# Stacked scores, packed values and a moved projection in the attention round of a two-block kernel

## What is computed

```python
h = xn @ w_in
b_c, c_c, h_c, q, k, v, g_conv, g_attn = jnp.split(h, list(splits), axis=-1)
y_conv = b_c * causal_dwconv(c_c * h_c, conv_w_mix)
...
# stick-breaking attention: 16 heads of 64, strictly causal
z = jnp.einsum("bqhd,bkhd->bhqk", qb, kb) * scale
log_beta = jax.nn.log_sigmoid(z)
log_fail = jnp.where(causal, log_beta - z, 0.0)
survive = lax.cumsum(log_fail, axis=3, reverse=True) - log_fail
a = jnp.where(causal, jnp.exp(log_beta + survive), 0.0)
o = jnp.einsum("bhqk,bkhd->bqhd", a, vb)
```

## Time and profile before

| | us |
|---|---|
| median of 3 runs (lowest to highest) | 1988.21 (1986.0 to 1995.19) |
| the profiled execution | 1980.69 |
| its span in the trace | 1979.0 |
| PE busy in the span | 1809.9 (91%) |
| DVE, ACT, POOL busy | 1096.1 (55%), 883.7 (45%), 227.3 (11%) |
| the eight rounds, first score to the last gap of the stage | 53.3 to 521.1 |

### The profile page before, as it was taken

The page is one execution under the profiler, slowest core; times in us unless marked ns, Lnnn a source line. Parts: engine busy times, 40 slices in busy tenths (PEclk is TensorE's granted clock), DMA queues, the critical chain, the costliest instruction groups (busy, mean ns, idle before and its releaser), DMA issues.

```text
span 1979.0 us, 31110 instructions
## 1 busy us (share of the span) xinstructions
PE 1809.9 (91%) x11965; PEld 1597.1 (81%) x11965; DVE 1096.1 (55%) x1580; ACT 883.7 (45%) x1157; POOL 227.3 (11%) x347
## 2 busy tenths in 40 slices
PE   5999999999999996999999968477879999999996
PEld 4899999999999995899888836366657777778884
DVE  4455445555333347554542277999677767654543
ACT  4565665666433344333332233134455565643332
POOL 0011111010000010000000007687000000000001
PEclk8999899999999998999999989799989999999998
DMA  3222122222223261232233228211202122133332
GB/s 121 77 83 67 53 85 74 75 74 83 63 90 95 90 197 43 88 95 95 85 98 96 93 101 139 38 40 46 76 22 86 59 74 69 48 106 112 123 101 96
DMA packets 64721, 166.02 MB, mean 84 GB/s; under 512 B 21956, under 2 KB 22148, under 8 KB 64520
## 3 DMA queue, kind: packets, MB, share of 16 engines
q1 hardware_dynamic: 64648, 165.03, 27.8%
HBM read 154.23 MB, written 8.41 MB: 82 GB/s over the span
## 4 chain that ended last, share of the span: by engine, by line
PE 71%; DVE 20%; ACT 4%; issue 3%; DMA 1%; SPq 0%; DVEq 0%; ACTq 0%; POOL 0%
PE J L749 32%; PE J L986 13%; PE J L761 6%; PE J L957 6%; PE J L866 3%; PE Z L821 2%; DVE WL L1687 2%; PE J L1153 2%; PE Z L833 1%; DVE VR L1963 1%; DVE VI L1963 1%; PE J L1104 1%; PE ZT L777 1%; DVE TS L1963 1%; DVE MX L2227 1%
## 5 line engine op out<-in xcount | busy, mean ns | idle before, releaser
L1687 DVE TENSOR_TENSOR WL<-WR,WH 128x1024 fp32r<-128x1024 f32 x271 | 337.3, 1245 | 328.8 <-ACT WH L1232 319.3
L1232 ACT ACTIVATE WH<-WR 128x1024 fp32r<-128x1024 f32 x271 | 285.6, 1055 | 220.8 <-DMA WR<-weights 76.0
L749 PE MATMUL J<-XH,WH 128*128 128x264 f32 (+1 forms) x1376 | 285.8, 289 | 22.9 <-DVE XL L1691 18.8
L749 PE MATMUL J<-XL,WH 128*128 128x264 f32 (+1 forms) x1376 | 281.4, 286 | 0.0
L749 PE MATMUL J<-XH,WL 128*128 128x264 f32 (+1 forms) x1376 | 281.0, 286 | 0.0
L749 PEld LDWEIGHTS J<-XH,WH 128*128 128x128 f32 x1376 | 217.4, 191 | 27.8 <-issue 17.1
L749 PEld LDWEIGHTS J<-XL,WH 128*128 128x128 f32 x1376 | 216.4, 191 | 0.0
L749 PEld LDWEIGHTS J<-XH,WL 128*128 128x128 f32 x1376 | 215.6, 191 | 0.0
L2371 POOL TENSOR_TENSOR SA<-SQ 128x512 f32<-128x512 f32 (+1 forms) x3 | 3.9, 1295 | 1018.4 <-ACT SQ L1463 511.4
L2352 POOL TENSOR_SCALAR_AFFINE_SELECT E<-E 128x128 f32<-128x128 f32 (+1 forms) x160 | 50.9, 354 | 460.1 <-DVE E L1754 246.5
L986 PE MATMUL J<-X2H,WH 128*128 128x512 f32 x168 | 70.8, 421 | 11.1 <-DVE X2L L2008 8.8
(11 more groups left out here) (435 smaller groups left out, 4334.5 us busy)
## 6 DMA issues: line engine op xcount, KB each, us to landing
WR<-weights SPq DMA_DIRECT2D x271, 512.0 KB, 3.5
X<-tokens SPq DMA_DIRECT2D x4, 528.0 KB, 5.5
H<-tokens SPq DMA_DIRECT2D x8, 264.0 KB, 4.2
res_dram<-H SPq DMA_DIRECT2D x1, 2048.0 KB, 8.1
u_dram<-UT SPq DMA_DIRECT2D x8, 256.0 KB, 2.2
US<-u_dram SPq DMA_DIRECT2D x16, 128.0 KB, 7.2
gate_dram<-GST SPq DMA_DIRECT2D x8, 256.0 KB, 2.2
GSB<-gate_dram SPq DMA_DIRECT2D x8, 256.0 KB, 3.7
```

The lines of the kernel that those rows point to most:

```text
L749: mm = pe.matmul(o[:, 512 * h:512 * h + half], ws[:, s, w], xs[:, a:a + half], start=(k == 0 and i == 0), stop=(k == 7 and i == 2))
L1232: act.activation(WH[:, n % SPLIT, :], WR[:, n % RAW, :], ACT.Copy).then_inc(w_hi, 1)
L1687: dve.tensor_tensor(WL[:, n % SPLIT, :], WR[:, n % RAW, :], WH[:, n % SPLIT, :].bitcast(F32), ALU.subtract).then_inc(w_lo, 1)
```

## The change

It does four things.

**Scores.** q's high and low half are stacked on the partitions of one operand per head (QS, 128 rows), k's high half is written twice (KS, 128 rows), so one pass gives high by high + low by high. A second pass over 64 rows adds the low half of k. 12 matmuls per head in place of 18, all of the first pass ahead of all of the second.

**Values.** The high and low half of a head's v stand side by side in one stationary operand (VW), so that the upper 64 output rows hold the low part. 18 matmuls per head in place of 27. The two halves of the output have to be added: ACT copies the one to OT (`head_part`), DVE adds the other (`head_sum`), ACT makes OH from OT, and DVE OL (`head_lo`).

**Copies.** q is read out by two instructions of 64 rows on ACT and two on DVE, k by four on ACT and two on DVE, where each was one.

**Order.** PE does job, then values(h-1); and job q, then values(h), then job k. The turns are: q t + 10, values(h) t + 11, k t + 12; in the first half the job has t + 5 and values(h-1) t + 6. On ACT and DVE the readers follow: q is read out before the values, both after `softplus(h + 1)`.

```diff
-                for kt, t0, w, c in PIECES:
-                    for ks, qs in ((KH, QH), (KH, QL), (KL, QH)):
-                        mm = pe.matmul(Z[:, c:c + w], ks[r, kt * P:(kt + 1) * P], qs[r, t0:t0 + w],
-                                       start=c // 512 not in banks, stop=True, skip_group_check=True)
-                        banks.add(c // 512)
+                    mm = pe.matmul(Z[:, c:c + w], KS[h % 2][:, kt * P:(kt + 1) * P], QS[h % 2][:, t0:t0 + w],
+                                   start=c // 512 not in banks, stop=True, skip_group_check=True)
+                    banks.add(c // 512)
+                for kt, t0, w, c in PIECES:
+                    mm = pe.matmul(Z[:, c:c + w], KL[r, kt * P:(kt + 1) * P], QS[h % 2][r, t0:t0 + w],
+                                   start=False, stop=True, skip_group_check=True)
...
-                    for vs, ps in ((VH, AH), (VH, AL), (VL, AH)):
-                        mm = pe.matmul(o[:, at + a:at + b], vs[:, kt * P:(kt + 1) * P], ps[:, c + a:c + b],
+                    for ps in (AH, AL):
+                        mm = pe.matmul(o[:, at + a:at + b], VW[:, kt, h % 2].rearrange("p x d -> p (x d)"), ps[:, c + a:c + b],
...
                 scores(h)
+                job(n + 1, t + 5, XH, XL)
                 if m.base or m.reg is not None:
-                    values(h - 1, t + 5)
-                job(n + 1, t + 6, XH, XL)
+                    values(h - 1, t + 6)
+                pe.wait_ge(read_out[slot(t + 4)], nth(t + 4) + 1)
                 turn_values(t + 7)
...
                 scores(h + 1)
+                if last:
+                    job(n + 6, t + 10, XH, XL, start=LIVE, half=HALFK)
+                else:
+                    job(n + 6, t + 10, XH, XL)
                 pe.wait_ge(read_out[slot(t + 7)], nth(t + 7) + 1)
-                values(h, t + 10)
+                values(h, t + 11)
                 if last:
-                    job(n + 6, t + 11, XH, XL, start=LIVE, half=HALFK)
                     job(n + 7, t + 12, XH, XL, start=LIVE, half=HALFK)
                 else:
-                    job(n + 6, t + 11, XH, XL)
                     job(n + 7, t + 12, XH, XL)
```

More of the change, by code:

```diff
@@ L175, in t_gate @@
     m = as_lin(m)
-    return T_GATE + (-1, 0, 1, 3)[j] if m.reg is None and m.base == 0 else T_GATE + 4 * m + j
+    return T_GATE + (-2, 0, 1, 3)[j] if m.reg is None and m.base == 0 else T_GATE + 4 * m + j
 def t_zs(m):
@@ L204, in halves, with heads @@
     return ap.rearrange("p (h t) -> p h t", h=2)
+def heads(ap):
+    return ap.rearrange("p (k x d) -> p k x d", x=2, d=64)
 def build(nc, weights, cond, params, tokens, bmat, cmat, positions, out):
@@ L580, in stream, with store_mod @@
                 repeat(sp, (last - first) // RAW, 1, lambda i: load_weights(first + RAW * i))
-            def store_mod(first, width, done):
+            def store_mod(first, width, done, rows=MROW):
                 sp.wait_ge(mod_rows, val(done))
-                sp.dma_start(mod_dram[:, cols(first, width)], MROW[0:2, 0:width]).then_inc(mod_saved, 16)
+                sp.dma_start(mod_dram[:, cols(first, width)], rows[0:2, 0:width]).then_inc(mod_saved, 16)
             def load_row(n, row):
@@ L1247, in _ @@
             act.activation(NONE[:], STAGE[:, 1, :], ACT.Copy, scale=-1.0).then_inc(const_r, 1)
-            act.activation(KH[:, L1:], STAGE[:, 1, 0:KPAD - L1], ACT.Copy, scale=0.0).then_inc(zeroed_act, 1)
+            act.activation(KS0[:, L1:], STAGE[:, 1, 0:KPAD - L1], ACT.Copy, scale=0.0).then_inc(zeroed_act, 1)
             act.activation(KL[:, L1:], STAGE[:, 1, 0:KPAD - L1], ACT.Copy, scale=0.0).then_inc(zeroed_act, 1)
@@ L1266, in _ @@
             root(0)
+            act.activation(KS[1][:, L1:], STAGE[:, 1, 0:KPAD - L1], ACT.Copy, scale=0.0).then_inc(zeroed_act, 1)
             for m in range(DT):
@@ L1365, in mix @@
                 softplus(h + 1)
-                head_out(h, m, t + 10)
+                if not last:
+                    q_hi(m + 1, t + 10, n + 6)
+                head_part(h, t + 11)
                 fail_hi(h + 1)
+                head_out(h, m, t + 11)
                 if not last:
-                    q_hi(m + 1, t + 11, n + 6)
                     split_hi(n + 10)
@@ L1737, in q_lo @@
                 dve.wait_ge(qk_hi, val(2 * m + 1))
-                dve.scalar_tensor_tensor(out=halves(QL[:]), in0=JV[as_lin(t) % 2], scalar=0.125,
-                                         in1=halves(QH[:]).bitcast(F32),
-                                         op0=ALU.mult, op1=ALU.subtract).then_inc(read_out[as_lin(t) % 2], 1)
+                for x in range(2):
+                    r, other = slice(64 * x, 64 * x + 64), slice(64 - 64 * x, P - 64 * x)
+                    ins = dve.scalar_tensor_tensor(out=halves(QS[x][other]), in0=JV[as_lin(t) % 2][r], scalar=0.125,
+                                                   in1=halves(QS[x][r]).bitcast(F32), op0=ALU.mult, op1=ALU.subtract)
+                ins.then_inc(read_out[as_lin(t) % 2], 1)
             def k_lo(m, t):
+                dve.wait_ge(k_first, val(m + 1))
+                low(halves(KL[0:64, 0:L1]), JV[as_lin(t) % 2][0:64], halves(KS[0][0:64, 0:L1]))
                 dve.wait_ge(qk_hi, val(2 * m + 2))
-                low(halves(KL[:, 0:L1]), JV[as_lin(t) % 2], halves(KH[:, 0:L1])).then_inc(read_out[as_lin(t) % 2], 1)
-            q_lo(0, T_MIX + 1)
+                low(halves(KL[64:P, 0:L1]), JV[as_lin(t) % 2][64:P], halves(KS[1][64:P, 0:L1]))\
+                    .then_inc(read_out[as_lin(t) % 2], 1)
+            q_lo(0, T_MIX)
             split_lo(SPLIT)
@@ L1835, in mix @@
                 low(YL[:, cols(m * L1, L1)], CT[:], YH[:, cols(m * L1, L1)]).then_inc(y_lo, 1)
-                head_out(h, m, t + 10)
+                if not last:
+                    q_lo(m + 1, t + 10)
+                head_sum(h, t + 11)
                 fail_lo(h + 1)
+                head_lo(h, m)
                 if not last:
-                    q_lo(m + 1, t + 11)
                     split_lo(n + 10)
```

93 lines of the change are left out of this document (58 added, 35 removed).

## The result

| | before | changed |
|---|---|---|
| median of the runs, us | 1990.31 (4 runs, 1986.0 to 1995.19) | 2013.82 (4 runs, 2007.49 to 2017.42) |
| ratio to before, 95% interval | | 1.0117 [1.0088, 1.0146] |
| span of the profiled execution, us | 1979.0 | 2005.5 |
| mean granted clock of TensorE in it | 0.968 | 0.957 |

The changed kernel is 1.2% slower: 23.5 us in the medians, 26.5 us between the two profiled spans. The forecast was 2001 us with a range up to 2012, so the sign was right and the size too small: the measured median lies 2 us above the range.

A forecast was written before the change was run, and what follows sets the result against it. PE, busy throughout the rounds, was taken to bound the kernel; its savings would become idle time before job k. 1980.7 + 0.6 (rounds, edges) + 12 (clock) = 1993.3 us profiled; as median 1988.2 + 12.6 = 2000.8, stated as 2001, range 1986 to 2012.

The forecast's parts named there:

- first round: First round of the stage: CT gap and low clock go, 59.45 to 57.4 us, -2.0; clock loss behind job k's gap added.
- LL and k's four copies: Around accumulate: LL stays hidden by 1 to 2 us, k's copies by 0.1 to 0.4, otherwise some 0.3 us a round.
- the forecast's two rows, of 2.64 and 2.81 us: Profiled gaps on PE before the change: clock fell behind 2.64 us, losing 1.7 us, but stayed at 1.00 behind 2.81.
- the single gap of 1.48 us: PE's wait for the first KL before the change: clock stayed at 1.00, so nothing was added for small idle times.
- Edges (b): Start: PE's 1.48 us wait for the first KL grows by three copies of 0.5 us, +1.4.
- softplus(h+1) starts at 321.15 + 0.1: Fifth round on ACT: softplus stays behind YH, only 0.1 us later, though its scores finish 3 us earlier.
- round +0.2: Each round: job k starts at 330.3 against 330.13, so the round takes 57.2 us; five undisturbed rounds, +1.0.
- the clock, 1.7 us in seven of eight: Behind the gaps ahead of job k: low clock costs 1.7 us each in seven of eight, +12 us; bounds none and 20.
- Rival 3: Worse: low stretches cost 2.5 us each, k's copies come out behind accumulate, (d) is not hidden; 2016 us, chance 0.12.
- (d): Third round: clock at 0.50 for 9.5 us without a gap cost 4.7; job k's gap absorbs it, -4.4.
- Last round: Second gate job waits for the first gate's sigmoid, +4.3; the stage's last gap adds +0.3, together +4.6.
- Rival 4: Faster: softplus(h+1) follows its scores, not YH; 1968 us, or 1957 if job k never waits for q; chance 0.11.

The follow-up runs named there:

- Experiments 2, 3 and 5: Groups of runs: 2 took order and forms apart (e3_order_alone, e4); 3 moved softplus or q's readout (e5, e2); 5 removed the wait (e7, e8).
- e2: Changed kernel with q read out in the middle of softplus(h+1), ahead of its last pass, on ACT and DVE; 1994.45 us, ratio 1.0018.
- experiment 1: Changed kernel with 30, 15 or 22 unused matmuls filling the wait before job k (e1, e11_fill_15, e12); 1999.64, 1995.4 and 2000.2 us.
- e11_fill_15: Changed kernel with 15 unused matmuls between values(h) and job k in each round; 1995.4 us in one execution.
- e4: Changed kernel's stacked scores and packed values in the order, turns and places of the kernel before; 1979.19 us, ratio 0.9940.
- e6_start: Changed kernel with the program's first q put in the other tile, as before the change; 2007.41 us, ratio 1.0086.
- e1: Changed kernel with 30 unused matmuls between values(h) and job k in each round; 1999.64 us, ratio 1.0050.
- e5: Changed kernel with ACT's copy of y (YH) put behind softplus(h+1); 2002.15 us, ratio 1.0049.
- e12: Changed kernel with 22 unused matmuls between values(h) and job k in each round; 2000.2 us in one execution.
- e3_order_alone: Kernel before with only the new order and turns, keeping its old three-pass scores and values; 2001.24 us, ratio 1.0037.
- e8: Changed kernel with e7's order and tiles, plus y put behind softplus and q's readout on ACT and DVE; 1952.08 us, ratio 0.9792.
- e9: e8's order with the kernel before's forms: three-pass scores and values and the old readouts; 1975.59 us, ratio 0.9917.
- e7: Changed kernel with q and k in different tiles, values(h) behind both, and the first gate's sigmoid directly behind softplus; 1964.14 us, ratio 0.9853.
- e10: e8 with packed values alone: scores back to three passes with the old copies of q and k; 1964.95 us, ratio 0.9864.

## Why the prediction was right in its mechanism and wrong in its size

Its terms against the two profiled executions, in us; the kernel's stage is cut at the same matmuls in both:

| part | forecast | measured |
|---|---|---|
| start, to the first scores (53.34 to 59.38) | +1.4 | +6.0 |
| first round (59.46 to 59.35) | -0.3 | -0.1 |
| rounds 2 to 7 (346.72 to 359.57) | +6.8 | +12.85 |
| last round to the last gap (61.59 to 68.69) | +4.6 | +7.1 |
| sum | +12.6 | +25.9 |

Of the 13.3 us missed, 4.6 lie at the start, 6.1 in rounds 2 to 7 (4.0 of it the chain to job k, the rest mostly the clock) and 2.5 in the last round, where it is all clock.

**Right.** Job k waits for q's readout behind softplus(h+1), PE idles from 37.8 us of the round (forecast 37.6), and what PE saved lies in that wait. Experiments 2, 3 and 5 show the cause: without the forms the wait is 0.9 us with the same round at full clock, with q's readout earlier (e2) job k begins earlier, and without the shared tile the wait is gone and so is the loss. LL and k's four copies stayed hidden: there is no gap behind accumulate. The clock falls behind these gaps, and experiment 1 shows what that is worth by itself. The Trainium skill's oscillation rule (TensorE: Matmul & The Clock Gate, "HAM oscillation — how this bites in real kernels"), by which every burst behind a wait starts cold, agrees with all seven waits of 4.2 to 4.8 us here; the six of 2.8 to 3.0 us in e11_fill_15 did not do it. The waits that the section describes are longer than those six, so neither they nor the forecast's two rows, of 2.64 and 2.81 us, tell for or against it. The Trainium skill's second rule, in the section "A second HAM failure mode: psum-queue depth-cycling" of the same page, is on small idle times that come often, and the single gap of 1.48 us by which the forecast had set it aside did not test it. It is borne out by the pairs of short waits in three rounds of e2 and not by those in the other four, nor by the waits of 1.1 and 1.6 us in e4, which lie 27 to 30 us apart.

**Wrong: "Edges (b)".** The step took one wait at the start, for KL, and made it 1.4 longer. Its own rule, q and k in one tile, holds for the first k job too, and it was not applied there: 3.06 us of wait at 42.74, all of which e6_start gives back. The wait for KL came out at 3.30 (+1.8, three copies by 0.6 and not 0.5), and the clock was low for about 3 us behind it (0.81 for the first pair instead of 0.51): from that row to the first scores it is 7.23 us against 6.04, another 1.2. 3.06 + 0.4 + 1.2 are the 4.6 us missed. It was luck that it was no more: in e1, e2, e5 and e12, which have the same two waits, the clock was low behind the wait for QS too, and the first scores came at 62.9 to 63.4 us (counted from the last wait for XL, at 38.73, it is 24.3 us in e1 against 21.5 here).

**Too small: "softplus(h+1) starts at 321.15 + 0.1", round +0.2.** Job k begins 0.83 us later in the round than before, not 0.2. Softplus is 0.40 late instead of 0.1: in the first half OL, which before was done in the shadow of POOL's masks, now stands between GL and the weight work, which begins at 15.63 us of the round against 15.03, and the loads (20.54 for the one at 319.64, against 308.43 - 288.46 = 19.97 before) and CT follow. The two q instructions begin 0.73 behind YL and not 0.61, take 1.42 together and not 1.31, and job k begins 0.14 behind them; the step had nothing there. 0.3 + 0.12 + 0.11 + 0.14 is the 0.66 by which 41.84 was missed. e3_order_alone shows that the order alone makes a chain of this length.

**Too small: the clock, 1.7 us in seven of eight.** The mean over rounds 2 to 7 is 59.93 - 57.04 - 0.85 = 2.0 us, and e1_fill gives 1.8. The price was read off one low stretch behind one gap of 2.64 us; behind 4.7 to 4.8 us they are longer in part: of rounds 2 to 7 (59.3 to 60.8 us, 57.9 of it without the clock) three paid 1.4 to 1.6 and three 2.3 to 2.9. The clock of the 12 us behind job k's start tells the same: 0.88, 0.85 and 0.87 in the first three, which is some 2.9 to 3.6 us at the lower level, and 0.79, 0.74 and 0.77 in the others, some 5 to 6. What decides between the two was not found. The last round's 8.05 us paid too. Rival 3's total, 2016, is 2 us from the measured one by luck: the clock cost 2.0 us a round and not its 2.5, the copies of k stayed hidden, and the 4.4 us of (d) did not come back; what it lacked was the start and the chain.

**(d)**, the third round's low stretch: the changed kernel's rounds have none that does not begin in a gap, so the 4.4 us were rightly taken off; whether they were hidden or did not occur can't be told. Such a stretch is no trait of the kernel before alone: the third round of e3_order_alone, with TensorE busy throughout from 200 to 210 us, had a clock of 0.88 there and took 60.0 us.

**Last round.** 7.1 for 4.6. The late start of the second gate job was forecast right: it begins 524.08 - 478.30 = 45.78 us into the round, where before it was 501.04 - 459.52 = 41.52, so 4.3 later. What is missing is the clock behind that wait: from the job's start to accumulate it is 8.24 us against 5.77, 2.5 more, which the table counts only in the seven rounds ahead.

**Rival 4** needed the softplus to follow its scores. e5_y_late shows it tied to y first, and 1.0 us ahead of that to AL. Its last sentence, all saved if job k does not wait for q (1957 us), is near what e8 does: 1952, 36 us less than before in the medians. The two profiled executions differ by 27.2 us, 32.5 at the stage's last gap: 33.4 saved in the first seven rounds and 0.9 at the start, and 1.7 lost in the last round. Some of the 33.4 is the order's own (e9).

## What to carry to other kernels

When passes are taken from a full engine, look for the first instruction behind them that another engine releases, and give it something else to wait for; the saved time is real only where that release comes early enough. Here the same two forms came out at -2.1% in one order of jobs and +1.2% in another, and what differed first was which two jobs share a tile: -1.5% with q and k in different tiles, values behind both and the gate's sigmoid earlier (e7). And apply the rule that one finds for the loop (here: two jobs in one tile) to the copy of the code ahead of the loop as well. If a wait on TensorE can't be removed, its length matters beyond itself: partly filled, it cost 1.8 us less a round than whole (e1). In two pieces of 1.1 and 1.6 us the clock stayed up (e4), but two pieces of 0.9 to 1.0 and 1.6 us, 7.7 us apart, brought it down in three rounds of seven (e2).

## What the runs showed of the hardware

- The granted clock follows no single gap length in these runs. It stayed at 1.00 behind six waits of 2.8 to 3.0 us (e11_fill_15) and behind the 3.06 us at 42.74 of the changed kernel (0.51 and then 0.40 a pair); behind the same 3.06 us at the same place it fell in e1, e2, e5 and e12 (0.81 and then 0.64 a pair). It fell behind all waits of 3.5 us and more before job k, behind 3.05 us there in e5 (0.64 over the next 4.7 us), behind 2.64 us in the kernel before, behind 2.23 us at the start of e3 (0.67 over 5.1 us), behind 2.84 us at the stage's last gap, behind 1.44 us there in e3 (0.71 over 5.8 us; the same 1.44 us left it at 1.00 in the kernel before), and in e2 behind waits of 1.03 and 1.55 us, 7.7 us apart, for about 10 us; a like pair in another round did nothing.
- Matmuls with no use, put into a wait, made the kernel some 13 us faster (1.0117 to 1.0050).
- Two DVE instructions on 64 rows that write to other rows than they read took 1.42 us together (0.71 each), as much as two of 0.70 on 128 rows: half the rows save nothing. The same holds for ACT's copies, 0.60 us on 128 rows and 0.61 on 64.
- Stacking two passes of scores over 64 rows into one over 128 saved 0.8 us a head (e10 against e8), not the third of 2.88 us.
